# TensorE sums two tiles of the last stage, and one borrowed weight slot moves up in the load order

## The reference, cut to what matters

```python
for i in range(2):
    h = h + mixer_i(rms_norm(h, norm_mix[i]))
    x = rms_norm(h, norm_ffn[i])
    # top-1 group, top-2 experts in it; gate is the product of the two weights
    h = h + sum over chosen experts of gate * (silu(x @ w_gate) * (x @ w_up)) @ w_down
y = h * rsqrt(mean(h*h) + 1e-6) * norm_final
```

## Time and profile before

| | |
|---|---|
| median of 3 timed runs | 1129.04 us (1127.11 to 1130.96) |
| the profiled execution, time | 1125.21 us |
| the profiled execution, span | 1123.4 us |
| PE / DVE / ACT / POOL busy, share of the span | 91% / 38% / 20% / 23% |
| mean granted TensorE clock | 0.976 |
| moved by DMA | 282.15 MB, mean 251 GB/s |

### The profile page before, as it was taken

The page is one execution under the profiler, slowest core; times in us unless marked ns, Lnnn a source line. Parts: engine busy times, 40 slices in busy tenths (PEclk is TensorE's granted clock), DMA queues, the critical chain, the costliest instruction groups (busy, mean ns, idle before and its releaser), DMA issues.

```text
span 1123.4 us, 17603 instructions
## 1 busy us (share of the span) xinstructions
PE 1021.5 (91%) x6710; PEld 728.5 (65%) x6710; DVE 429.3 (38%) x1386; ACT 224.3 (20%) x703; POOL 258.5 (23%) x413
## 2 busy tenths in 40 slices
PE   7999999998999998879999899999998999998970
PEld 6777777885555555468767687677896555554540
DVE  1234454443333332243253533434464333432326
ACT  4334442001000000022123232332311000000002
POOL 3612332001222221123121221212211122221213
PEclk9999999999999999999999999999998999998995
DMA  9413040679999999986311202227068999999996
GB/s 310 120 52 113 1 188 27 242 259 355 415 418 417 419 417 422 401 308 204 104 52 59 90 31 95 68 95 302 24 241 296 364 419 418 418 415 420 417 391 240
DMA packets 73335, 282.15 MB, mean 251 GB/s; under 512 B 10410, under 2 KB 37114, under 8 KB 47200
## 3 DMA queue, kind: packets, MB, share of 16 engines
q1 hardware_dynamic: 58768, 249.31, 56.4%
q0 software_dynamic: 14480, 31.65, 8.0%
HBM read 268.66 MB, written 28.70 MB: 265 GB/s over the span
## 4 chain that ended last, share of the span: by engine, by line
PE 79%; DMA 11%; DVE 4%; issue 2%; ACT 2%; POOL 1%; SPq 0%; POOLq 0%; ACTq 0%; DVEq 0%
PE ps L1817 22%; PE ps L2121 17%; PE ps L1809 11%; PE ps L2133 8%; DMA area<-in_w_up 8%; PE ps L2106 3%; PE ps L2353 2%; PE ps L1789 2%; PE ps L2319 2%; PE ps L2128 2%; PE ps L1880 1%; PE ps L2002 1%; PE ps L2017 1%; DMA area<-y_scratch 1%; PE ps L2032 1%
## 5 line engine op out<-in xcount | busy, mean ns | idle before, releaser
L1817 PE MATMUL ps<-area 128*128 128x256 f32 x1152 | 265.8, 383 | 5.1 <-ACT area L895 2.5
L2121 PE MATMUL ps<-area 128*64 128x256 f32 x976 | 227.9, 387 | 19.0 <-DMA area<-in_w_up 13.7
L1817 PEld LDWEIGHTS ps<-area 128*128 128x128 f32 x1152 | 213.9, 191 | 35.4 <-issue 4.8
L2122 PE MATMUL ps<-area 128*64 128x256 f32 x944 | 220.9, 388 | 0.0
L2121 PEld LDWEIGHTS ps<-area 128*64 128x64 f32 x976 | 131.0, 139 | 84.4 <-issue 21.7
L695 POOL DMA_INDIRECT y_scratch<-area,idx_i x64 | 63.8, 997 | 335.2 <-DVE area L1497 289.5
L2122 PEld LDWEIGHTS ps<-area 128*64 128x64 f32 x944 | 127.0, 139 | 0.0
L1809 PE MATMUL ps<-area 128*128 128x272 f32 x512 | 123.4, 396 | 0.0
L2133 PE MATMUL ps<-area 128*64 128x512 f32 x236 | 114.2, 607 | 4.4 <-issue 3.7
L1482 DVE SCALAR_TENSOR_TENSOR area<-ps,area 64x256 f32<-64x256 f32 x64 | 31.4, 491 | 223.1 <-ACT area L990 223.1
L2134 PE MATMUL ps<-area 128*64 128x512 f32 x236 | 114.2, 607 | 0.0
(11 more groups left out here) (245 smaller groups left out, 1207.1 us busy)
## 6 DMA issues: line engine op xcount, KB each, us to landing
area<-in_w_gate SPq DMA_DIRECT2D x61, 1024.0 KB, 24.7
area<-in_w_up SPq DMA_DIRECT2D x59, 1024.0 KB, 20.5
area<-in_w_down SPq DMA_DIRECT2D x59, 1024.0 KB, 27.4
area<-in_w_b_qkv SPq DMA_DIRECT2D x12, 1024.0 KB, 8.8
area<-y_scratch SPq DMA_DIRECT2D x8, 1024.0 KB, 10.1
area<-in_w_a_qkv SPq DMA_DIRECT2D x6, 1024.0 KB, 13.1
hid<-in_w_down SPq DMA_DIRECT2D x6, 1024.0 KB, 21.5
hid<-in_w_up SPq DMA_DIRECT2D x6, 1024.0 KB, 28.5
```

The costliest lines, as they stand in the source:

```text
L1817: ins = nc.tensor.matmul(ps[:r, bank, at_col:at_col + F], x[:, k, COL[t]:COL[t] + r], w[:, k, :], start=k == k0, stop=k == k1 - 1)
L2121: nc.tensor.matmul(ps[0:CAP, bank, 0:F], x[:, k, :], wg[:, k, :], start=k == 0, stop=k == KD - 1)
L2122: ins = nc.tensor.matmul(ps[CAP:P, bank, 0:F], x[:, k, :], wu[:, k, :], start=k == 0, stop=k == KD - 1)
```

## The change

Four things change. (1) In the last stage, tiles 0 and 2 (`SUM_PE`) are summed by TensorE in PSUM: identity times `hid`, then for each expert a diagonal matrix of the gates times its rows. POOL makes the diagonals. DVE keeps three combines; ACT's square and `y_rows` read PSUM for the two. (2) `y_rows` writes each tile to a place of its own, and no longer waits for an output. (3) H1 waits for tiles 2 and 3 alone; the two `y_out` semaphores now count tiles 2 and 3, and the others. (4) H1 stands ahead of R0 to R3 in `MOE_SLOTS`.

```diff
-MOE_SLOTS = [["N0", "N1", "F5", "F6", "R4", "R5", "S0", "F0", "F1", "F2", "F3", "F4", "W0", "R0", "R1", "R2", "R3", "X0", "X1", "H1", "M", "H0"]] * 2
+MOE_SLOTS = [["N0", "N1", "F5", "F6", "R4", "R5", "S0", "F0", "F1", "F2", "F3", "F4", "W0", "H1", "R0", "R1", "R2", "R3", "X0", "X1", "M", "H0"]] * 2
...
-        if name[0] == "H":
-            return [(y_flip, NT * (2 * layer + 2)), (sumsq, NT * (2 * layer + 2))] + \
-                [(y_out[b], 16 * (3, 2)[b] * (layer + 1)) for b in range(2)]
+        if name == "H1":
+            done = 1 + max(LATE.index(2), LATE.index(3))
+            return [(y_flip, NT * (2 * layer + 1) + done), (sumsq, NT * (2 * layer + 1) + done), (y_out[0], 16 * 2 * (layer + 1))]
+        if name == "H0":
+            return [(y_flip, NT * (2 * layer + 2)), (sumsq, NT * (2 * layer + 2)), (y_out[1], 16 * 3 * (layer + 1))]
...
+    def sum_ps(i):
+        b = 2 * SUM_PE.index(i)
+        return ps[:, b:b + 2, :].rearrange("p b c -> p (b c)")
...
+            if layer:
+                for i in SUM_PE:
+                    sp.wait_ge(tile_in[TILES[4][i]], 64)
+                sp.sem_inc(prepared, 1)
             for b in range(2):
                 sp.wait_ge(scat[b], NE // 2 * (layer + 1) * 16)
...
+        pool.wait_ge(ye_sb, 2 * NE)
+        for i in SUM_PE:
+            t = TILES[4][i]
+            for c in range(2):
+                ins = nc.gpsimd.tensor_scalar(gate_diag[i][c], ident, gw[:, c, t:t + 1], 1.0, ALU.mult, ALU.mult)
+        ins.then_inc(prepared, 1)
         for i in range(NT):
             norm_small(4, i)
...
-            if i >= 2:
-                dve.wait_ge(final_out[i % 2], 16 * (i // 2))
-            nc.vector.scalar_tensor_tensor(ynorm[n][i % 2][:r, :], hid[:r, t, :], rstd[:r, t:t + 1], gbc[:r, :],
+            rows = sum_ps(i) if i in SUM_PE else hid[:r, t, :]
+            nc.vector.scalar_tensor_tensor(yfin[i][:r, :], rows, rstd[:r, t:t + 1], gbc[:r, :],
                                            ALU.mult, ALU.mult).then_inc(y_ready, 1)
...
         combine(1, TILES[4][0])
-        for i in range(NT):
-            if i + 1 < NT:
-                combine(1, TILES[4][i + 1])
-            y_rows(4, i)
+        y_rows(0)
+        combine(1, TILES[4][2])
+        y_rows(1)
+        combine(1, TILES[4][4])
+        for i in range(2, NT):
+            y_rows(i)
...
+        pe.wait_ge(prepared, 8)
+        for i in SUM_PE:
+            t = TILES[4][i]
+            rows = sum_ps(i)
+            for h in range(2):
+                cols = slice(OUT_HALF * h, OUT_HALF * h + OUT_HALF)
+                nc.tensor.matmul(rows[:, cols], ident, hid[:, t, cols], start=True, stop=False)
+        idle_products(2)
+        for i in SUM_PE:
+            t = TILES[4][i]
+            pe.wait_ge(tile_in[t], 80)
+            rows = sum_ps(i)
+            for h in range(2):
+                cols = slice(OUT_HALF * h, OUT_HALF * h + OUT_HALF)
+                for c in range(2):
+                    ins = nc.tensor.matmul(rows[:, cols], gate_diag[i][c], y2b[t][:, c, cols], start=False, stop=c == 1)
+            ins.then_inc(summed, 1)
```

More of the change, by code:

```diff
@@ L69 @@
 LATE = [4, 3, 2, 1, 0]
+SUM_PE = (1, 3)
 TILES = [[0, 1, 2, 3, 4], LATE, [0, 1, 2, 3, 4], LATE, [4, 0, 1, 2, 3]]
@@ L312, in program @@
     gbc = part(R_G, D)
+    yfin = [part(R_R + D * i, D) for i in range(NT)]
+    gate_diag = {i: [part(R_R + NT * D + P * (2 * n + c), P) for c in range(2)] for n, i in enumerate(SUM_PE)}
     root_of = part(R_G, N)
@@ L386, in program @@
     y_out = [sem(f"y_out{i}") for i in range(2)]
-    final_out = [sem(f"final_out{i}") for i in range(2)]
+    final_out = sem("final_out")
     hid_attn = sem("hid_attn")
     hid_moe = sem("hid_moe")
+    summed = sem("summed")
     roots = sem("roots")
@@ L493, in oT_ready @@
         return at["ab"[layer], "o"], NT * (k_end // 2 - 1) + LATE.index(t) + 1
+    SUM_DVE = [i for i in range(NT) if i not in SUM_PE]
+    def sum_ps(i):
+        b = 2 * SUM_PE.index(i)
+        return ps[:, b:b + 2, :].rearrange("p b c -> p (b c)")
     block = ctx.enter_context(nc.Block())
@@ L598, in _ @@
             sp.wait_ge(y_ready, 2 * NT + i + 1)
[L599 to L602, removed]
+            sp.dma_start(O[0][0, COL[t]:COL[t] + P, :] if t < 4 else O[1][0], yfin[i][:ROWS[t], :]) \
+              .then_inc(final_out, 16)
+        sp.wait_ge(final_out, 16 * NT)
     @block.gpsimd
@@ L622, in rows_out @@
             pool.wait_ge(hid_attn, OUT_DONE[n // 2][t])
-            pool.dma_start(hn_dram[COL[t]:COL[t] + r, :], hid[:r, t, :]).then_inc(y_out[i % 2], 16)
+            pool.dma_start(hn_dram[COL[t]:COL[t] + r, :], hid[:r, t, :]).then_inc(y_out[t not in (2, 3)], 16)
         def g_load():
@@ L712, in moe @@
             for b in range(2):
-                pool.wait_ge(y_out[b], 16 * (3, 2)[b] * (layer + 1))
+                pool.wait_ge(y_out[b], 16 * (2, 3)[b] * (layer + 1))
             wait_apart(pool, r_idx, 2 * layer + 1)
@@ L847, in _ @@
         moe(1)
+        pool.wait_ge(ye_sb, 2 * NE)
[4 more added lines that the diff above has]
+        ins.then_inc(prepared, 1)
         for i in range(NT):
             norm_small(4, i)
-        pool.wait_ge(y_out[0], 16 * 6)
-        pool.wait_ge(y_out[1], 16 * 4)
+        pool.wait_ge(y_out[0], 16 * 4)
+        pool.wait_ge(y_out[1], 16 * 6)
         pool.wait_ge(k_out, 16 * 6)
@@ L866, in square @@
                 act.wait_ge(hid_attn, OUT_DONE[n // 2][t])
+            elif n == 2:
+                act.wait_ge(hid_moe, i + 1)
+            elif i in SUM_PE:
+                act.wait_ge(summed, SUM_PE.index(i) + 1)
             else:
-                act.wait_ge(hid_moe, NT * (n // 2 - 1) + i + 1)
+                act.wait_ge(hid_moe, NT + SUM_DVE.index(i) + 1)
             if n or i:
                 act.wait_ge(sumsq, NT * n + i)
-            nc.scalar.activation(junk[n][:r, :], hid[:r, t, :], ACT.Square, accum_out=ss[:r, t:t + 1]) \
+            rows = sum_ps(i) if n == 4 and i in SUM_PE else hid[:r, t, :]
+            nc.scalar.activation(junk[n][:r, :], rows, ACT.Square, accum_out=ss[:r, t:t + 1]) \
                 .then_inc(sumsq, 1)
@@ L1135, in _, with y_rows @@
         own = Link(dve_own)
-        def y_rows(n, i):
-            t = TILES[n][i]
+        def y_rows(i):
+            t = TILES[4][i]
             r = ROWS[t]
-            dve.wait_ge(rstd_ready, NT * n + i + 1)
+            dve.wait_ge(rstd_ready, NT * 4 + i + 1)
             if i == 0:
                 dve.wait_ge(g_in, 64)
-            if i >= 2:
-                dve.wait_ge(final_out[i % 2], 16 * (i // 2))
-            nc.vector.scalar_tensor_tensor(ynorm[n][i % 2][:r, :], hid[:r, t, :], rstd[:r, t:t + 1], gbc[:r, :],
+            rows = sum_ps(i) if i in SUM_PE else hid[:r, t, :]
+            nc.vector.scalar_tensor_tensor(yfin[i][:r, :], rows, rstd[:r, t:t + 1], gbc[:r, :],
                                            ALU.mult, ALU.mult).then_inc(y_ready, 1)
```

## The result

The changed kernel took 1119.07 us (median of 11 runs, 1115.26 to 1124.69); the kernel before, timed beside it, 1128.09 (11 runs, 1126.76 to 1130.96). The ratio is 0.9923, 95% interval 0.9907 to 0.9938: 8.7 us faster, 7.0 to 10.5. Timed again on another chip the ratio was 0.994, 0.992 to 0.996. The profiled execution took 1117.58 us, its span is 1115.7 (before 1123.4).

The account below looks back on a forecast made before the run. The last stage was taken as bound by DVE, ACT and POOL with a load floor, the experts' start by the first gather. 3.7 (last stage) + 1.2 (slot) = 4.9 us off 1129.04 gave 1124.1, range 1119.5 to 1128.0.

Parts of the forecast that it names:

- The last stage: Final combines and y_rows: two combines leave DVE, last y_rows starts at 1115.35 instead of 1119.05; 3.7 us gained, bounds 3.1 to 4.35.
- SP's new wait: SP's queue before the last stage: waiting for reloaded hid tiles 0 and 2, landed by 1093.9, before 1096.2; booked at nothing.
- TensorE's price: Last stage: 0.45 us per 512-column product, doubled at half clock; four products after a load lands take 1.8 to 3.6 us.
- the short price: POOL's second small operation in the last stage: 0.55 us where DVE is idle, against 1.43 beside a combine.
- The 0.6 us that the prediction saw: Last stage: by the port rule, PSUM-reading y_rows spare POOL, so the last could start at 1114.7; 0.6 us extra, not summed.
- the slot's 1.2 us: Experts' start: moving H1's megabyte from in front of the first gather gains 0.4 us in layer 0 and 0.8 in layer 1.
- the upper bound of 2.3: First gathers of both layers: most the slot could gain, 1.0 us each plus 0.3 more for layer 1.
- rival 1: Experts' start, layer 1: a shorter gather wait may keep TensorE's clock, 2.8 us more, 7.7 gained in all, 1121.3; chance 0.14.
- 2: Experts' start: the clock falls in layer 0 too, leaving a gain of 2.1 us, 1126.9; chance 0.05.
- 3: Slot does nothing, and slow POOL pairs and dearer PSUM y_rows eat part of the tail; gain 2.3 us, 1126.7; chance 0.24.
- 4: Slower, 1133: H1's wait holds SP's queue beyond 3.4 us slack in layer 1, or TensorE's sums come 7 us late; chance 0.05.
- 5: First gathers: the skill's fixed-cost fit gives 3.2 us each, gaining 4.3 us there, 8.0 in all, 1121.0; chance 0.04.

Follow-up runs that it names:

- 8 idle products: Changed kernel with 8 idle products instead of 12 ahead of each layer's experts: 1121.94 us, against the changed kernel's 1117.71 beside it.
- the slot alone: Kernel before plus only H1 ahead of R0, waiting for tiles 2 and 3 alone; last stage as before. Run twice: 1123.03 and 1121.71 us.
- the 16 idle products: Kernel before with 16 idle TensorE products instead of 12 ahead of each layer's experts: 1123.43 us, 2.8 faster than before.
- the last stage alone: Kernel before plus only the TensorE sums and the separate y_rows places; slot order and H1's waits as before: 1121.47 us, 5.6 faster.
- 13 and 14 in the changed kernel: Changed kernel with 13 idle products in layer 0 and 14 in layer 1 instead of 12: 1118.95 us, against the changed kernel's 1117.71 beside it.

## Why the prediction was wrong

**The last stage: right in size, but for one wait in its path.** 3.7 us were booked, 3.6 to 3.7 measured. As walked through were the wait of 2 us ahead of `y_rows(0)`, the eleven operations, the last `y_rows` 15.9 us after the first combine (forecast about 16), the four identity products (and the two idle ones) hidden behind tile 0's load but for 0.3 us, and SP's new wait, which was free. Not as walked through was the end. The prediction had the sum of tile 2 waited for by nothing, and the last `y_rows` by tile 3's square and POOL. In the trace the chain runs through tile 2's sum: its `y_rows` (1110.09) waits 0.44 us for POOL, and the last one (1111.29) for nothing. Both paths end at nearly the same time, so the size came out.

**TensorE's price: the right number by luck.** I read "x24" as 24 products, and so 0.45 us for one of 512 columns, and took 3.6 for a sum because the clock would be at half. The 24 are two matmuls for each of 12 float32 products: four products of 512 columns show as x8. A product of 512 columns costs 0.9 us at the full clock, 3.6 for the sum, and the clock was full. The lower bound, 1.8 us, could never have come. Of the work on the sums only the four identity products (from 1092.12) ran at a lowered clock, under cover. The windows of the changed kernel:

```profile
1092.00:1096.00 4.00, 3.88 (x6) 1.70 (x6) 0.57 (x1) 0.00 (x0) 0.07 (x1) 0.57 0.70 227
1096.00:1100.00 4.00, 4.00 (x13) 2.22 (x12) 1.98 (x2) 1.15 (x2) 0.64 (x2) 1.00 1.01 420
1100.00:1104.00 4.00, 2.91 (x8) 1.12 (x7) 3.75 (x3) 1.15 (x3) 1.11 (x2) 1.00 1.02 424
```

**POOL beside DVE: the short price where PSUM is read.** In the changed kernel the second small operation took these times:

```profile
1104.07 0.56 POOL L630 TENSOR_TENSOR small<-small 128x1 f32<-128x1 f32 x1
...
1105.48 0.55 POOL L630 TENSOR_TENSOR small<-small 128x1 f32<-128x1 f32 x1
...
1108.59 1.47 POOL L630 TENSOR_TENSOR small<-small 128x1 f32<-128x1 f32 x1
...
1110.42 0.55 POOL L630 TENSOR_TENSOR small<-small 128x1 f32<-128x1 f32 x1
```

The 1.47 stands beside a `y_rows` out of `hid` (1108.38), the 0.55 at 1105.48 and at 1110.42 beside those out of `ps` (1104.66, 1110.09). That agrees with the port rule of the Trainium skill ("SBUF — State Buffer", who interferes with whom), by which a DVE instruction with two SBUF inputs holds up a GpSimd one that reads SBUF. The 0.6 us that the prediction saw in it did not come: the 1.47 lies on the chain that ended last, beside the one `y_rows` there that reads `hid`. The last `y_rows` started 15.9 us after the first combine, where the short price would have given 15.1.

**The failed step: the slot's 1.2 us, and the clock at nothing.** Two terms of the sum were too small.
- *The gathers, mis-sized.* I booked 0.4 and 0.8 by guessing how much of H1's megabyte was left when the gather went out. They gave 1.2 and 1.1, the upper bound of 2.3 in sum. The step "little of it was left in layer 0" was wrong: the 5.9 us between load and gather had to hold X0 and X1's megabytes too, which went out just ahead of H1; three megabytes take some 7.5 us at 420 GB/s, and from 252 to 255 the engines were 0.97 busy, where the changed kernel shows 0.27. Over the thirteen profiles a first gather 4.4 to 6.1 us behind H1's load took 5.2 to 6.5 us in six cases of seven (the seventh 4.5), one 6.8 or 6.9 us behind it 4.4, 4.4 and 4.6, and one with H1 long gone 3.9 to 4.5. Experts 0, the piece that scatters least, says the same in its length: 224.2 to 224.9 us in the five profiles with the slot's edit and a kept clock (X0 and X1 in place), 225.8 to 226.2 in the three with the old slots and a kept clock, 228.0 and 229.1 in the two where 8 idle products or the old slots went with a fallen one. That is some 1.4 for the gather and 3 to 3.5 for the clock, in one layer.
- *The clock, left out.* "Against it: 0.8 is little" was the wrong sentence in rival 1. The wait got 1.2 us shorter, to 0.94, and in both profiles of the changed kernel the clock is kept. Rival 1 said 7.7 in sum; with the gathers at 2.3 it would have said 8.8, against 8.7 and 6.8 measured.

The base of the forecast adds to the miss: 1129.04 was the median of three times, and the eleven times of the comparison give 1128.09. By the medians the gain is 9.0 us, inside the 9.5 on which the lower end of the range rested.

**Is the clock's 2.8 us shown?** That a fallen clock costs something near it is: behind a fallen clock it took 7.35 to 8.6 us from the first transposes to N0's reuse, with a kept one 5.6 to 5.7; the changed kernel with 8 idle products paid 3 to 4 us for two layers with nothing else changed; and the idle products alone gained 2.8 (0.6 to 5.1) in the kernel before, a shorter gather in its profile among it. That each timed execution of before has it fallen in layer 1, and none of the changed one, is not. The mean granted clock of whole executions is 0.9735 for before (35 runs), 0.9738 and 0.9748 for the slot alone, 0.975 for the 16 idle products. A stretch of some 8 us at half clock in one layer would be 4 in 1123, 0.0036, and the differences are smaller. But that mean doesn't settle it: the profile of before, with its clock fallen behind the wait, has 0.976, and both profiles of the slot alone, with theirs kept, have 0.974, since the clock falls in other stretches too, as in the router's. What is left is the time: the slot alone gained 3.3 and 4.2 us, less 2.3 for the gathers, which leaves 1 to 2 us for the clock on average, an estimate with intervals of some 2 us to either side; how often it falls in before stays open. (The last stage's edit raises the mean by itself, to 0.9815, since TensorE works there now.)

**Rivals.** 2 (a clock that falls in layer 0 too) was seen in the last stage alone. 3 is out: the slot gained, and POOL's pair was short beside the reads of PSUM. 4 was right in its mechanism, and is what the new place costs without the narrower wait; here its 3.4 us of slack were not used up, R0 went at 828.60. 5, the Trainium skill's fit ("DMA: Bandwidth & Descriptors", anatomy of one DMA), gave an estimate of 3.2 us for a gather; no first or second gather here, over thirteen profiles, came under 3.8, and with nothing ahead of it the first took 4.0 and 4.3. The estimate is 0.6 us or more too low for this gather.

## What to carry to other kernels

A megabyte that moved from in front of a gather into idle time of the DMA engines was worth the whole excess of that gather over the best one in the same trace, and it wasn't taken from the stream. Look at the DMA engines' share in the window in which the gather goes out, and count all loads that are queued there, before guessing what is left of one; when the queue holds more than it can drain, book the upper bound. In this kernel a wait of TensorE near 2 us had a second price behind it, the half clock: look at the granted clock behind each such wait, and ask first whether the change makes it shorter or longer. Count the products in the program, not the "x" in a row, before a price for one is taken from it: a float32 product is two matmuls there. A profile holds other things that scatter: here the clock in the router's stretch, worth as much as what was being measured.

## What the runs showed of the hardware

- The clock fell behind every wait of 1.97 us and more at the experts' start (1.97, 2.09, 2.25, 2.33, 2.59, 3.04, 4.91 and 5.29), and stayed behind each of 1.72 and less (1.72, 1.03, 0.95, 0.94 twice, and shorter ones), over thirteen profiles. With 16 idle products, or 13 and 14 in the changed kernel, it was kept in every profile (three). I had thought 0.8 us off such a wait too little to matter.
- The clock also fell ahead of the experts, in the router's stretch, where TensorE's longest wait in layer 1 is 0.83 us in all thirteen profiles: in layer 1 in eight of them (down to 0.50, between 848 and 858), whose attention was 0.5 to 3.5 us longer than that of the other five; in layer 0 in twelve, and the thirteenth (16 idle products in the kernel before) sent its first gather at 251.2, the others at 252.1 to 255.4. Why it falls in some executions only stays open.
- The same gather of 128 rows (512 KB) took 3.9 to 4.5 us with nothing fresh in front of it, 5.2 to 6.5 with H1's megabyte 4.4 to 6.1 us ahead (4.5 once), and 8.4 to 8.7 with seven megabytes ahead: a long queue of loads doesn't hold it back in proportion.
- A 128x1 operation of POOL took 0.55 us beside a DVE operation that reads PSUM and SBUF, and 1.43 and 1.47 beside one that reads two tiles of SBUF.
